# mLSTM heads 1 to 3 with split probabilities, head 0's state split around a unit, and state stores in another place of the queue

## The reference

```
def mlstm_chunkwise(q, k, v, log_i, log_f, C0, n0, m0):
    ...
        S = jnp.einsum('bhtd,bhsd->bhts', qc, kc) * jnp.exp(Dm - m_t[..., None])
        num = inter[..., None] * jnp.einsum('bhtk,bhkv->bhtv', qc, C) + jnp.einsum('bhts,bhsv->bhtv', S, vc)
        den = inter * jnp.einsum('bhtk,bhk->bht', qc, n) + jnp.sum(S, axis=-1)
        h = num / jnp.maximum(jnp.abs(den), jnp.exp(-m_t))[..., None]
        ...
        C_new = scale[..., None, None] * C + jnp.einsum('bhsk,bhsv->bhkv', kw, vc)
        n_new = scale[..., None] * n + jnp.sum(kw, axis=2)
```

## Time and profile before

| what | value |
|---|---|
| median of three runs | 1884.65 us (1881.69 to 1885.49) |
| profiled execution, its own time | 1882.92 us |
| its span | 1881.2 us |
| TensorE busy | 1842.8 us (98%) |
| VectorE, ScalarE, GpSimd busy | 970.4, 781.1, 742.2 us |
| TensorE's granted clock | 0.993 of full |

### The profile page before, as it was taken

One profiled execution on the slowest core, in us unless ns is written; L12 is line 12 of the kernel. 1 busy time (PEld: TensorE's weight loads), 2 busy tenths in 40 slices (PEclk: granted clock), 3 DMA queues, 4 the chain that ended last, 5 costly groups with the idle time before them and its releaser, 6 DMA issues.

```text
span 1881.2 us, 33626 instructions
## 1 busy us (share of the span) xinstructions
PE 1842.8 (98%) x13546; PEld 1726.9 (92%) x13546; DVE 970.4 (52%) x1305; ACT 781.1 (42%) x1223; POOL 742.2 (39%) x622
## 2 busy tenths in 40 slices
PE   7999999999999999999999999999999999999997
PEld 7999999999999999998566665999999999999997
DVE  6787645524634522697776667322255336426313
ACT  4576835322322334443543444423454323323333
POOL 3333554352342344565232312554644433422541
PEclk9999999999999999999999999999999999999999
DMA  4222232322322322422389779322233222333221
GB/s 131 85 84 75 90 97 73 91 89 84 86 89 85 90 79 79 98 70 99 132 272 309 235 265 310 92 85 72 86 101 96 90 85 81 90 87 86 85 82 65
DMA packets 187435, 210.71 MB, mean 112 GB/s; under 512 B 24611, under 2 KB 150179, under 8 KB 187247
## 3 DMA queue, kind: packets, MB, share of 16 engines
q1 hardware_dynamic: 187074, 208.71, 36.1%
q10 hardware_dynamic: 224, 0.07, 0.0%
HBM read 168.09 MB, written 40.64 MB: 111 GB/s over the span
## 4 chain that ended last, share of the span: by engine, by line
PE 85%; DVE 5%; ACT 3%; DMA 2%; POOL 2%; issue 2%; SPq 0%; ACTq 0%; DVEq 0%; POOLq 0%
PE ps L2571 40%; PE ps L2714 23%; PE ps L2694 11%; DMA out_ml_C_s_dram<-C_HALVES 2%; PE ps L2955 2%; PE ps L3054 1%; PE ps L3016 1%; PE ps L2994 1%; PE ps L2889 1%; POOL W_LO L768 1%; DVE H_PAD L1903 1%; POOL K_LO L1005 1%; POOL V_LO L1013 1%; DVE C_HALVES L2376 1%; PE ps L3004 0%
## 5 line engine op out<-in xcount | busy, mean ns | idle before, releaser
L768 POOL TENSOR_TENSOR W_LO<-W_RAW,W_HI 128x512 fp32r<-128x512 f32 x392 | 545.2, 1402 | 555.5 <-ACT W_HI L1091 532.0
L1091 ACT ACTIVATE W_HI<-W_RAW 128x512 fp32r<-128x512 f32 x412 | 254.1, 628 | 500.7 <-PE ps L2571 257.5
L2571 PE MATMUL ps<-A_HI,W_HI 128*128 128x288 f32 x1144 | 247.5, 298 | 6.8 <-DVE A_LO L1739 4.8
L2571 PE MATMUL ps<-A_HI,W_LO 128*128 128x288 f32 x1144 | 245.7, 297 | 0.0
L2571 PE MATMUL ps<-A_LO,W_HI 128*128 128x288 f32 x1144 | 245.5, 297 | 0.0
L2571 PEld LDWEIGHTS ps<-A_HI,W_HI 128*128 128x128 f32 x1144 | 185.1, 190 | 9.3 <-issue 6.7
L2571 PEld LDWEIGHTS ps<-A_LO,W_HI 128*128 128x128 f32 x1144 | 185.3, 190 | 0.0
L2571 PEld LDWEIGHTS ps<-A_HI,W_LO 128*128 128x128 f32 x1144 | 185.2, 190 | 0.0
L871 POOL TENSOR_TENSOR G_LO<-GATED,G_HI 128x1152 fp32r<-128x1152 f32 x22 | 58.9, 2675 | 236.8 <-ACT G_HI L1335 236.6
L2714 PE MATMUL ps<-A_HI,W_HI 128*128 128x288 f32 x576 | 123.4, 296 | 0.0
L2714 PE MATMUL ps<-A_HI,W_LO 128*128 128x288 f32 x576 | 123.4, 296 | 0.0
(11 more groups left out here) (469 smaller groups left out, 4111.6 us busy)
## 6 DMA issues: line engine op xcount, KB each, us to landing
W_RAW<-in_ffn_w_up_dram SPq DMA_DIRECT2D x176, 256.0 KB, 2.8
C_HALVES<-in_state_mlstm_C_dram SPq DMA_DIRECT2D x64, 512.0 KB, 5.3
out_ml_C_s_dram<-C_HALVES SPq DMA_DIRECT2D x64, 512.0 KB, 5.4
W_RAW<-in_ffn_w_down_dram SPq DMA_DIRECT2D x88, 256.0 KB, 2.8
W_RAW<-in_ml_w_in_dram SPq DMA_DIRECT2D x64, 256.0 KB, 2.7
W_RAW<-in_rg_w_in_dram SPq DMA_DIRECT2D x48, 256.0 KB, 2.7
W_RAW<-in_ple_w_gate_dram SPq DMA_DIRECT2D x32, 256.0 KB, 2.8
W_RAW<-in_ml_w_out_dram SPq DMA_DIRECT2D x32, 256.0 KB, 2.9
```

The costliest lines, as they stand in the source:

```text
L768: pool.tensor_tensor(W_LO[:, s], W_RAW[:, s], W_HI[:, s].bitcast(F32), ALU.subtract).then_inc(lo_ready, 1)
L1091: act.activation(W_HI[:, s], W_RAW[:, s], ACT.Copy).then_inc(hi_ready, 1)
L2571: ins = pe.matmul(ps[:, 4 * s + 2 * m + h, 0:HALF_T], a[:, w, k, wc], x[:, h * HALF_T:h * HALF_T + HALF_T], start=i == 0 and k == 0 and q ...
```

## The change

It has five parts.

- In heads 1 to 3 ScalarE copies the four pieces of PROBS to fp32r (PROBS_HI1 to 3, laid where the inputs of earlier heads were), and GpSimd subtracts (PROBS_LO, in place of PROBS). V_LO is made early too, right after the key tokens.
- In these heads a block of weighted values is three fp32r passes over the four pieces instead of one fp32 pass, and the denominators are two passes with ONES_R, a copy of the ones in fp32r.
- In head 0 the state block 0 is split: its two passes with V_HI stand before unit 5, the pass with V_LO behind it.
- SyncE stores state blocks 0, 1 and 2 in steps 11, 13 and 14 instead of 10, 12 and 14, in all heads; in step 11 the store stands behind the row loads.
- In head 3 VectorE's first subtraction for the next stage (`xn_lo(0, ...)`) stands behind the squares.

```diff
@@ def hybrid_trunk (SyncE) @@
-                    if v in (10, 12, 14):
-                        store_cp(h, v // 2 - 5)
+                    if v in (11, 13, 14):
+                        store_cp(h, {11: 0, 13: 1, 14: 2}[v])
@@ (GpSimd) @@
+            def probs_lo(h):
+
+                for n, i in enumerate((0, 1, 3, 2)):
+                    cols = slice(PROBS_AT[i], PROBS_AT[i + 1])
+                    pool.wait_ge(probs_high, 4 * (h - 1) + n + 1)
+                    pool.tensor_tensor(PROBS_LO[:, cols], PROBS[:, cols], P_HI_OF[h][:, cols].bitcast(F32), ALU.subtract).then_inc(probs_low, 1)
...
                 pool.wait_ge(v_high, h + 1)
-                pool.wait_ge(piece_done, DONE[h, "pv3"])
+                if not h:
+                    pool.wait_ge(piece_done, DONE[h, "pv3"])
...
                 if h:
                     key_tokens(h)
+                    values_lo(h)
+                    probs_lo(h)
...
                 keys_lo(h)
-                values_lo(h)
+                if not h:
+                    values_lo(h)
@@ (ScalarE) @@
+            def probs_hi(h):
+
+                for i, name in ((0, "sc0"), (1, "sc13"), (3, "sc13"), (2, "sc2s")):
+                    cols = slice(PROBS_AT[i], PROBS_AT[i + 1])
+                    act.wait_ge(bank_freed[at(h, name)], FREED[h, name, at(h, name)])
+                    act.activation(P_HI_OF[h][:, cols], PROBS[:, cols], ACT.Copy).then_inc(probs_high, 1)
...
             values_hi(0)
+            act.activation(ONES_R[:, :], ONES[:, :], ACT.Copy).then_inc(ones_ready, 1)
...
+                    probs_hi(h)
                 weighted_keys(h)
@@ (VectorE) @@
                     normalise(h - 1, SEQ, N_STOK, 2 * h)
-                    if h == HEADS - 1:
-                        xn_lo(0, G_MIX + 8, A_HI, A_LO)
...
                 square_mean(h, "hp", 0, 0, SEQ)
                 if h == HEADS - 1:
+                    xn_lo(0, G_MIX + 8, A_HI, A_LO)
                     xn_lo(2, G_MIX + 8, A_HI, A_LO)
@@ (TensorE) def weighted @@
+                if h:
+                    if v == 0:
+                        pe.wait_ge(probs_high, 4 * h)
+                        pe.wait_ge(v_low, 4 * h + 4)
+                    cols = slice(v * P, v * P + P)
+                    for part in range(3):
+                        if v == 0 and part == 2:
+                            pe.wait_ge(probs_low, 4 * h)
+                        for i in range(4):
+                            own = slice(PROBS_AT[i], PROBS_AT[i + 1])
+                            a, b = ((v_hi(h, i)[:, cols], P_HI_OF[h][:, own]), (V_LO[:, i, cols], P_HI_OF[h][:, own]),
+                                    (v_hi(h, i)[:, cols], PROBS_LO[:, own]))[part]
+                            ins = pe.matmul(ps[:, bank, i * P:SEQ], a, b, start=i == 0 and part == 0, stop=i == 3 and part == 2)
...
@@ def denominators @@
+                if h:
+                    pe.wait_ge(ones_ready, 1)
+                    for part, t in enumerate((P_HI_OF[h], PROBS_LO)):
+                        for i in range(4):
+                            ins = pe.matmul(ps[:, bank, i * P:SEQ], ONES_R[:, :], t[:, PROBS_AT[i]:PROBS_AT[i + 1]],
+                                            start=i == 0 and part == 0, stop=i == 3 and part == 1)
...
@@ the heads' order @@
-                prompt_state(h, 0)
-                unit(h, 5)
+                if h:
+                    prompt_state(h, 0)
+                    unit(h, 5)
+                else:
+                    take(h, "cp0")
+                    states_of_high_values(h)
+                    unit(h, 5)
+                    prompt_state(h, 0)
```

## The result

The changed kernel takes 1915.07 us (median of four runs, 1912.48 to 1921.78) against 1885.07 for the kernel before (1881.69 to 1887.89): ratio 1.0165, 95% interval 1.0134 to 1.0196. It is 30 us slower. The forecast had the sign, but put the time at 1892.5 and the upper end of its range at 1899. The profiled execution has a span of 1913.3 us, 32.1 more than before.

A forecast was written before the change was run, and what follows sets the result against it. TensorE was taken to bound the kernel, until the DMA queue or a helper comes late. Gains of 6.7 us and waits of 15.5 sum to +8.8, giving 1891.7 or 1893.5; it said 1892.5, range 1883 to 1899.

The forecast's parts named there:

- What bounds the kernel: Whole program and the four mLSTM heads: TensorE bounds, with 85% of the chain, until the DMA queue or a helper is late.
- The wait itself: TensorE's wait near each head's end for ScalarE's copy behind the moved store: 4.7, 4.9, 4.9, 1.0, sum 15.5 us lost.
- Wait 4.9, twice: Heads 1 and 2, before state block 3: TensorE arrives at +18.7 after unit 4, may start at +23.6; 4.9 us lost each.
- the 6.7 gained: Heads 1 to 3: cheaper weighted values and denominators and no V_LO wait save 2.55 + 2.55 + 1.6 us.
- Weighted blocks and denominators: Heads 1 to 3: a weighted block falls from 2.26 to 1.96 us, the denominators from 2.26 to 1.28.
- Rival 3: Weighted values and denominators: 128-column fp32r products cost 0.25 us, like fp32; +4.5 us, 1896 to 1898; chance 10%.
- Unit 4: Heads 1 to 3, after the denominators: unit 4 waits 0.57 us for bank 0, leaving 0.4 a head of their saving.
- V_LO: Heads 1 to 3: made early by GpSimd, it ends TensorE's wait, 0.95 us a head; the splits cause no wait.
- Head 0's split worth nothing: Head 0, around unit 5: the split covers 0.95 us of wait, which turns into wait for unit 6's load; zero gain.
- In head 3 the third part does not arrive: Head 3, unit 7: the 0.95 us saved on the V_LO wait becomes 0.95 more wait for C_HALVES.
- Landing times: Stores of state blocks: measured 2.7 to 7.3 us, median 5.9; taken 5.7 in heads 1 and 2, not the skill's 2.6.
- Rivals 1 and 2: Moved stores: 1, landing in 2.7 us, 1882.5 to 1884, 10%; 2, the queue thins, 1876.5 to 1878, 10%.

The follow-up runs named there:

- the copies at the other place: Kernel before, with ScalarE's copy of the samples' numerators at the end of heads 0 to 2 made eleven times: 1895.94 us, 10.8 more.

## Why the prediction was wrong

- **What bounds the kernel, the place and cause of the loss: right.** Two lines in SyncE's queue, through ScalarE's copy to TensorE.
- **The wait itself: right.** 5.2, 4.9, 4.4 and 1.1 us against 4.7, 4.9, 4.9 and 1.0; sum 15.5 against 15.5. In head 1 two errors cancel: the store went 19.1 us after unit 4, not 17.2, and landed in 4.9, not 5.7, while TensorE came 1.2 later than I had it, with 1.56 of wait for C_HALVES at unit 6. In head 0 the store went 1.0 earlier than I had it and landed in 6.0, not 4.9. That the sum agrees to 0.1 is luck.
- **The step that failed: "Wait 4.9, twice", and the sum built on it, price a wait at its length.** The sum had no term for what follows a wait. Half clock followed, in TensorE's work for 15 to 16 us behind each of the three long waits. It cost 20.7 us, over twice the whole forecast change. In the profiled execution, where it was measured, the change costs 32.1: the forecast 8.8, these 20.7, and 2.7 of the 6.7 gained that did not arrive. In the run with products in the waits, the two executions that kept the clock are 9.9 and 10.8 above the kernel before, near the forecast's 8.8.
- The trace of before could have warned me. At the end of head 3 TensorE waits 1.42 us, and the window behind it has the clock at 0.66; I read the earlier trace rows, where it is 1.00, and looked no further. It would not have given the size: that is 3.4 us at half clock, under 2 us lost.

```profile
1174.79 0.37 PE L2555 MATMUL ps<-A_HI,W_HI 128*128 128x288 f32 x1 [1.42 <-ACT C_PROMPT L1561]
```

```profile
1170.00:1175.00 5.00, 3.58 (x19) 2.55 (x19) 2.52 (x4) 3.56 (x7) 0.00 (x0) 1.00 0.96 348
1175.00:1180.00 5.00, 5.00 (x28) 4.96 (x27) 4.96 (x4) 0.04 (x1) 3.48 (x3) 0.66 0.34 114
```

- **Weighted blocks and denominators: right.** 1.93 against 1.96, and 1.28 against 1.28. A pass of 1280 columns takes 0.645, which leaves 0.116 for the 128-column product (I took 0.10). Rival 3 falls.
- **Unit 4: right in kind.** 0.40 of wait, not 0.57.
- **V_LO: right, and the splits on ScalarE and GpSimd are free.** No wait for V_LO, PROBS_HI or PROBS_LO; only 0.23 to 0.26 us before the first weighted block in each of heads 1 to 3.
- **Head 0's split worth nothing: right**, by the run without it.
- **"In head 3 the third part does not arrive": too narrow.** It does not arrive whole in heads 1 and 2 either. TensorE waits there for C_HALVES too (1.56 and 0.53), 6.4 us in all where my steps gave 3.3; without the late stores the change is worth 4.0, not 6.7.
- **Block 1's move from step 12 to 13: left out.** In the changed kernel it costs nothing visible, since TensorE is late already. Once block 0's store is early, it costs 6 to 10 us (11.4 less 5.8, and 9.7 alone).
- **Landing times: right to take the measured ones.** The store in head 1 landed in 4.9 us, and the sixteen in 2.0 to 6.5, median 5.1. The Trainium skill's figure (DMA: Bandwidth & Descriptors, section "Anatomy of one DMA — SWDGE (gpsimd) path"), 2.6 us for 256 KB, lies near the shortest only. The page fits it to DMAs issued by GpSimd; these stores stand in SyncE's queue, so it was never a price for them.
- **Rivals 1 and 2** needed a quick landing or a thinner queue; the C store issued at 1030.09 landed in 6.3 us and the moved store, issued at 1039.28, in 4.9, which together is the 11 of the forecast and not under 6.

## What to carry over

Price a wait that you give TensorE in two terms: its length, and the work behind it at half clock. Here the second was on average 3 to 7 us for each wait of 1.4 to 5 us near a head's end, though nothing behind one of them (2.51 us), and under 1 us each among the next head's projections. So give it a range that starts at zero, look in the profile before for a wait near the same place and read the granted clock behind it. Where executions of one kernel differ, compare their mean clocks before you compare their times. And when you move one DMA issue in a shared queue, follow every store or load whose step changed to the buffer that it frees and to what stands behind the instruction that waits for it.

## What the runs showed of the hardware

- **Idle time of TensorE can be paid twice.** Behind the changed kernel's waits of 4.4 to 5.2 us the granted clock was 0.50 (1.2 GHz) for 15 to 16 us of full work before it came back to 1.00; filling these waits with 20 to 22 products that nobody reads kept it at 1.00. The Trainium skill (TensorE: Matmul & The Clock Gate, section "HAM oscillation — how this bites in real kernels") describes this for a loop whose wait for a DMA puts every round back to the low clock; behind these three waits the trace agrees (0.50 each time).
- **It is not a matter of length alone.** Waits of 1.0, 1.4 and 1.6 us near a head's end were followed by 0.50, but one of 2.5 by 1.00 (the stores moved in the kernel before, head 2), and two of 1.0 as well (block 0 first in step 11, block 1 late). Of nine waits of 1.8 to 3.4 us among the projections, six were followed by 1.00 and three by 3.4 to 6.8 us at 0.50 (2.69 and 3.44 with block 1 late alone, the third of 2.56 with the copies at the other place). And in three profiles the clock fell for 3.4 us at unit 3 with no wait before it, only behind the split weighted blocks. What TensorE does just before and after seems to count; no run here settles it.
- **A short wait can cost several times its length.** Four waits of 1.4 us, 5.5 in all, cost 19.2 us.
